# First-table blocks turned by TensorE from a ring of four whole-row tiles, and all sample tokens served by gathered rows and dots

## The reference

```python
q = (xb @ w_pq).reshape(T, PEER_HEADS, 2, D_HALF)
s = jnp.einsum('thcd,ckd->thck', q, sub_keys)
...
best, sel = lax.top_k(cand, PEER_TOPK)            # 8 heads x 16 = 128 experts of each token
eidx = jnp.take_along_axis(cidx, sel, axis=-1)
g = jax.nn.softmax(best, axis=-1)
u = jnp.take(u_tab, eidx, axis=0)                 # rows of the first table, 16384 x 2048
a = jax.nn.gelu(jnp.einsum('thkd,td->thk', u, xb))
vv = jnp.take(v_tab, eidx, axis=0)                # rows of the second table
return jnp.einsum('thk,thkd->td', g * a, vv)
```

## Time and profile before

| | |
|---|---|
| median of 3 runs | 2655.49 us (2642.95 to 2659.84) |
| the profiled execution, its own time | 2656.08 us |
| its span, first to last instruction | 2654.5 us |
| mean granted TensorE clock | 0.969 of full |
| until the first gelu of the U stage | 854.3 us |
| from the first gelu to the last (127 blocks) | 1016.5 us |
| from the last gelu of the U stage to the end | 783.7 us |

### The profile page before, as it was taken

How to read it: one execution, slowest core, us unless ns; L and a number is a source line. 1 busy time by engine, 2 the same in 40 slices (tenths; PEclk the granted TensorE clock), 3 DMA queues, 4 the chain that set the end, 5 groups by cost and what they waited for, 6 DMA issues and landing times.

```text
span 2654.5 us, 38865 instructions
## 1 busy us (share of the span) xinstructions
PE 2437.1 (92%) x13838; PEld 2178.1 (82%) x13838; DVE 1922.1 (72%) x2105; ACT 932.1 (35%) x1018; POOL 1171.8 (44%) x684
## 2 busy tenths in 40 slices
PE   5989999999799999999979898898998999999899
PEld 4878777788699999999979898898776777777777
DVE  4554654643567998989877776776588898888888
ACT  3354544522333333323322232222333333333333
POOL 1020101020000010177888888882676675767662
PEclk9999999999899999999989999998999999999999
DMA  5453544495355568689888998997899999999997
GB/s 184 132 186 112 174 129 135 150 380 190 81 119 122 163 199 224 183 230 220 212 235 231 264 245 231 237 241 202 304 390 390 399 385 411 387 391 406 394 398 301
DMA packets 280169, 661.43 MB, mean 249 GB/s; under 512 B 73145, under 2 KB 123129, under 8 KB 237912
## 3 DMA queue, kind: packets, MB, share of 16 engines
q1 hardware_dynamic: 154832, 334.57, 38.9%
q0 software_dynamic: 82064, 249.26, 27.7%
q10 hardware_dynamic: 43191, 76.58, 10.2%
HBM read 613.65 MB, written 46.02 MB: 249 GB/s over the span
## 4 chain that ended last, share of the span: by engine, by line
PE 36%; POOL 25%; DMA 15%; DVE 13%; issue 7%; DVEq 1%; ACT 1%; ACTq 1%; SPq 0%; POOLq 0%
POOL g_dense L500 16%; PE banks L1297 11%; PE banks L1298 11%; PE banks L1299 11%; POOL a_values L542 6%; DMA a_tile<-a_dense 4%; DVE h L1249 4%; DMA v_row<-in_v_tab,route_place 3%; DMA raw<-in_v_tab 3%; POOL u_row L494 2%; DMA v_raw<-in_v_tab 2%; DMA raw<-in_u_tab 2%; POOL v_row L533 1%; DVEq L847 1%; DVE u_turned L1126 1%
## 5 line engine op out<-in xcount | busy, mean ns | idle before, releaser
L1297 PE MATMUL banks<-xT_hi,ring_hi 128*128 128x320 f32 (+1 forms) x2304 | 737.2, 320 | 88.4 <-DVE ring_lo L1130 81.2
L1298 PE MATMUL banks<-xT_lo,ring_hi 128*128 128x320 f32 (+1 forms) x2304 | 731.3, 317 | 0.0
L1299 PE MATMUL banks<-xT_hi,ring_lo 128*128 128x320 f32 (+1 forms) x2304 | 730.8, 317 | 0.0
L500 POOL DMA_INDIRECT g_dense<-route,route_place x256 | 497.1, 1942 | 132.1 <-issue 76.2
L1297 PEld LDWEIGHTS banks<-xT_hi,ring_hi 128*128 128x128 f32 x2304 | 444.8, 193 | 98.6 <-issue 83.3
L1298 PEld LDWEIGHTS banks<-xT_lo,ring_hi 128*128 128x128 f32 x2304 | 444.9, 193 | 0.0
L1299 PEld LDWEIGHTS banks<-xT_hi,ring_lo 128*128 128x128 f32 x2304 | 444.1, 193 | 0.0
L533 POOL DMA_INDIRECT v_row<-in_v_tab,route_place x128 | 284.4, 2222 | 187.3 <-DVE h L1249 165.4
L868 DVE TENSOR_TENSOR ring_lo<-raw,ring_hi 128x2048 fp32r<-128x2048 f32 x72 | 164.8, 2292 | 252.7 <-ACT ring_hi L580 252.4
L1130 DVE TENSOR_TENSOR ring_lo<-u_turned,ring_hi 128x2048 fp32r<-128x2048 f32 x128 | 290.5, 2270 | 72.3 <-ACT ring_hi L785 71.8
L1126 DVE STREAM_TRANSPOSE u_turned<-raw 128x2048 f32<-128x2048 f32 x128 | 295.6, 2310 | 63.7 <-DMA raw<-in_u_tab 55.5
(11 more groups left out here) (219 smaller groups left out, 3791.6 us busy)
## 6 DMA issues: line engine op xcount, KB each, us to landing
raw<-in_u_tab SPq DMA_DIRECT2D x512, 128.0 KB
raw<-in_u_tab ACTq DMA_DIRECT2D x512, 128.0 KB
v_raw<-in_v_tab SPq DMA_DIRECT2D x64, 1024.0 KB, 10.8
raw<-in_v_tab SPq DMA_DIRECT2D x64, 1024.0 KB, 12.1
raw<-in_w_in SPq DMA_DIRECT2D x160, 256.0 KB
a_dense<-gelu_out SPq DMA_DIRECT2D x128, 160.0 KB
raw<-in_w_out SPq DMA_DIRECT2D x64, 256.0 KB
g_dense<-zeros POOLq DMA_DIRECT2D x16, 1024.0 KB, 28.9
```

What stands on the lines that cost most here:

```text
L500: pool.indirect_dma_start(out=places, out_offset=bass.IndirectOffsetOnAxis(ap=routeU[:, t, 2, j:j + 1], axis=0), in_=route[:, t, 0, j:j + ...
L1297: MM(out, h1, h2, start=first, stop=False)
L1298: MM(out, h1, l2, start=False, stop=False)
L1299: return MM(out, l1, h2, start=False, stop=last)
```

## The change

Blocks of the first table are now loaded as whole rows (8 KB a partition, one DMA a block, from SP alone) into four buffers instead of two. TensorE turns them, 16 transposes of 128x128 into four PSUM banks, in two halves of 8. They stand inside the matmuls of the block before. ACT and VectorE make the hi and lo part from PSUM, in two halves too. VectorE's `turn` and `u_turned` are gone, and with them the permuted layout of x and of `w_pq`.

The U stage's matmuls lose the 64 sample tokens: 256 columns instead of 320. All 128 sample tokens go by gathered rows: 128 gathers and 128 dots instead of 64, and no copies of x and indexes. The V stage has no `gather_gelus` left; `w_values` is made once.

GpSimd's order is new: tile 0 is routed first and its scatters begin; after 48 scatters there is one gather after every two scatters. The dots are spread over blocks 31 to 123.

```diff
-TILE_ORDER = (2, 0, 1)
-ALONE = N_SWEEPS + N_PARTS
-MIXED = ALONE + 3 * N_PARTS - 1
-GT = 64
-TU = T - GT
-DOTS = GT
+TILE_ORDER = (0, 2, 1)
+FIRST, SECOND = N_SWEEPS + N_PARTS, N_SWEEPS + 2 * N_PARTS
+TU = SEQ
+DOTS = PH * TOPK
+LAST_DOT = 124
 NUB = 3
+UR = 4
+AHEAD_ROWS = 48
...
 def dots_after(m):
-    if m < MIXED:
-        return max(m + 1 - ALONE, 0) // 3
-    done = (MIXED - ALONE) // 3
-    return min(DOTS, done + (m + 1 - MIXED) * (DOTS - done) // 66)
+    return min(DOTS, max(m + 1 - SECOND, 0) * DOTS // (LAST_DOT - SECOND))
...
-        u_v = I["u_tab"][0].rearrange("(r i q) (a d) -> a i q r d", r=4, i=32, q=P, a=4)
+        u_v = I["u_tab"][0].rearrange("(p q) d -> p q d", q=P)
...
+            def u_next(m, slot):
+                sp.wait_ge(u_turn, m * 2 + (2 - 2 * UR))
+                u_load(m, slot)
...
-            for n in range(TD // P * PH * 2):
-                t, h, half = n // (2 * PH), n // 2 % PH, n % 2
-                if n % (2 * PH) == 0:
-                    pool.wait_ge(rt_ready, t + 2)
-                if half == 0 and n:
-                    pool.wait_ge(g_scat, 16 * (n // 2 * TOPK))
-                for k in range(half * TOPK // 2, (half + 1) * TOPK // 2):
-                    scatter(t, h * TOPK + k)
-                while gathered < min(DOTS, dots_after(38 + (n + 1) * 5 // 2) + NUB):
+            for n in range(N_SCATTER // 2):
+                t, j = divmod(2 * n, SLOTS)
+                if j == 0:
+                    pool.wait_ge(rt_ready, 1 + 2 * t)
+                if j % TOPK == 0 and n:
+                    pool.wait_ge(g_scat, 16 * 2 * n)
+                scatter(t, j)
+                scatter(t, j + 1)
+                if 2 * n == AHEAD_ROWS:
+                    pool.wait_ge(rt_ready, 2)
+                if 2 * n >= AHEAD_ROWS and gathered < DOTS:
                     gather_dot(gathered)
                     gathered += 1
...
-            def gather_gelus(i):
...
             pool.wait_ge(rt_ready, NT)
+            pool.wait_ge(dot_done, DOTS)
             gather_row(0)
...
             def u_hi(m, k):
-                act.wait_ge(u_turn, m + 3)
...
+                for g in range(2):
+                    act.wait_ge(u_turn, 2 * m + g + 1)
+                    if m >= 2:
+                        act.wait_ge(u_used, m - 1)
+                    A(ringH[:, k, g * 2 * W:(g + 1) * 2 * W], psum[:, 2 + 2 * g:4 + 2 * g, :], ACT.Copy).then_inc(u_hi_done, 1)
...
-            for m in range(P - 2):
-                turn(m + 1, (m + 1) % 2)
+            for m in range(P):
                 u_lo(m, m % 2)
...
+            def u_turns(n, it, slot, g):
+                pe.wait_ge(u_in[slot], it * 16 + 16)
+                pe.wait_ge(u_lo_done, n * 2 + (g - 1))
+                for i in range(8):
+                    b = 8 * g + i
+                    last = TR(bank[2 + b // 4][:, b % 4 * P:(b % 4 + 1) * P], rawu[slot][:, b * P:(b + 1) * P], ident)
+                last.then_inc(u_turn, 1)
+
+            def u_step(m, it, q, turns=True):
                 pe.wait_ge(gelu_done, m + 1)
                 for b in range(KC):
+                    if turns and b in (2, 8):
+                        u_turns(m + 1, it + (q + 1) // UR, (q + 1) % UR, b // 8)
+                    if b % 8 == 0:
+                        pe.wait_ge(u_lo_done, m * 2 + (b // 8 + 1))
```

More of the change, by code:

```diff
@@ L278, in hybrid_layer @@
         g_zero, g_scat = sem("g_zeroed"), sem("g_scattered")
-        u_turn, gelu_done = sem("u_turn"), sem("gelu_done")
+        u_in = [sem(f"u_in{i}") for i in range(UR)]
+        u_turn, u_hi_done, u_lo_done, u_used, gelu_done = (sem(x) for x in "u_turn u_hi u_lo u_used gelu_done".split())
         a_store = [sem("a_store0"), sem("a_store1")]
@@ L338, in _, with u_load @@
                     weight_step(nb * 4 + (BASE_WOUT + i), i % 2, I["w_out"][0], kq, slice(nb * W, (nb + 1) * W))
-            pq = I["w_pq"][0].rearrange("(a b j) n -> a j b n", a=4, b=KC)
             with sp.Fori(0, 4) as nb:
                 for kq in range(4):
[L343 to L349, removed]
+                    weight_step(nb * 4 + (BASE_WPQ + kq), kq % 2, I["w_pq"][0], kq, ds(nb * W, W))
+            def u_load(m, slot):
+                sp.dma_start(rawu[slot], u_v[:, ds(m, 1), :].rearrange("p o d -> p (o d)")).then_inc(u_in[slot], 16)
+            def u_next(m, slot):
+                sp.wait_ge(u_turn, m * 2 + (2 - 2 * UR))
+                u_load(m, slot)
             def store_gelu(m, k):
@@ L354, in store_gelu @@
                 sp.dma_start(Ad[ds(m, 1), :, :].rearrange("o p x -> (o p) x"), aout[:, k, :]).then_inc(a_store[k], 16)
[L356 to L373, removed]
+            sp.wait_ge(split_used, BASE_WPQ + 2)
+            u_load(2, 2)
+            u_load(3, 3)
+            for m in range(2):
+                sp.wait_ge(lo_done, BASE_U + m + 1)
+                u_load(m, m)
+            for m in range(UR, 2 * UR):
+                u_next(m, m % UR)
+                if m >= 6:
+                    store_gelu(m - 6, m % 2)
+            with sp.Fori(2, P // UR) as it:
+                for q in range(UR):
+                    u_next(it * UR + q, q)
+                    store_gelu(it * UR + (q - 6), q % 2)
             def v_weights(m, slot):
@@ L521, in _ @@
                 gathered += 1
-            pool.wait_ge(dot_gelu, 1)
-            pool.dma_start(aval[own, 0:DOTS], adot[0:GT, :]).then_inc(aown_in, 16)
-            pool.dma_start(aval[own, DOTS:SLOTS], adot[own, :]).then_inc(aown_in, 16)
-            gelus = Ad.rearrange("m p (t o) -> (m p t) o", o=1)
             rows = I["v_tab"][0]
@@ L535, in gather_row @@
                     in_offset=bass.IndirectOffsetOnAxis(ap=routeU[:, NT - 1, 1, k:k + 1], axis=0)).then_inc(row_in[k % NVB], 16)
[L537 to L544 removed]
             pool.wait_ge(rt_ready, NT)
+            pool.wait_ge(dot_done, DOTS)
             gather_row(0)
[L548 to L553 removed]
+            pool.wait_ge(u_used, P)
             for k in range(1, SLOTS):
[L555 to L557 removed]
                 gather_row(k)
@@ L805, in _ @@
                 gelu(m, m % 2)
-                if m == P - 4:
-                    act.wait_ge(dot_done, DOTS)
-                    A(adot[:, :], adot[:, :], ACT.Gelu_apprx_tanh).then_inc(dot_gelu, 1)
-            u_hi(P - 1, 1)
-            gelu(P - 2, 0)
-            gelu(P - 1, 1)
             def v_hi(m, s, sets):
@@ L1215, in _ @@
                     dots += 1
-            turn(P - 1, 1)
-            u_lo(P - 2, 0)
-            u_lo(P - 1, 1)
             def w_product(j):
```

154 lines of the change are left out of this document (46 added, 108 removed).

## The result

The changed kernel takes 2683.73 us (median of 4 runs, 2683.65 to 2698.41), against 2654.01 for the kernel before on the same chip: the ratio is 1.0126, with a 95% interval of 1.0099 to 1.0153. It is slower by 1.3% on that ratio (the forecast was 2700, 1.7%). The profiled execution took 2683.65 us, its span is 2682.1.

What follows compares the result with a forecast made beforehand. TensorE, then VectorE's chain, bound the U stage before and transfers the V stage; GpSimd's list would bound the U stage's middle after. Span 2654.5 + 75 - 30, plus 1.6 around it, gives 2701, forecast 2700 us; 8-in-10 range 2630 to 2750.

Steps and rivals of the forecast that it cites:

- The bound: U stage, blocks 31 to 106: GpSimd's ordered list sets the pace, 9.2 us a block.
- the floor: U stage: TensorE's least time a block, 5.76 us of matmuls plus 1.76 of transposes, 7.52 us.
- Transposes cost more: Rival, U stage: transposes take 0.18 us each among fast matmuls, floor 8.7 us a block, 2757 us; chance 0.08.
- The cycle: GpSimd, middle of U stage: two scatters and a gather 4.99 us, dots 1.0, landing waits 0.5; 6.5 us a gather.
- Its place in the time: U stage timeline: first gather at 1093, 104th at 1769, end at 1946 us, 75 later than before.
- The rule on `u_lo`: U stage: `u_lo` with one input in PSUM doesn't hold GpSimd back; if wrong, up to 38 us more.
- The V stage: V stage: without small gathers in groups of eight, DMA goes at 410 GB/s instead of 393, saving 30 us.
- At nothing: The rest, costed at zero: SP's loads and four buffers, DMA demand of 275 GB/s, GpSimd's waits.
- it has 7 us to spare: SP's queue, U stage: a gelu's store stands behind a load that awaits a turning, with 7 us of slack.
- chain up: Rival, U stage: late gathers stop VectorE, TensorE idles and its clock falls; 15 to 45 us more, 2715 to 2745; chance 0.17.
- TensorE sets the pace: Rival, U stage: a GpSimd cycle under 5.46 us leaves TensorE as the limit, 2572 us; chance 0.08.

## Why the prediction was right

**The bound.** It named GpSimd's list as what sets the middle stretch, and three of the runs confirm it from three sides: another mix of the same list shortens it, wider matmuls don't lengthen it, shorter dots shorten it.

**TensorE.** 0.12 us for 256 columns and 0.11 for a transpose both hold, and so does the floor: 7.5 us a block in the first 31 blocks (7.52 said) and 7.4 in the last 21. "Transposes cost more" is out.

**The cycle.** Said: 4.99 of its own, 1.0 for the dots, 0.5 for landing, 6.5 in all. Measured: 1.2 at most for the dots, 33.3 / 103 = 0.3 for landing, 6.44 in all. A dot holds GpSimd somewhat longer than I took from the mean of all operations (a scatter begun under a dot ends 1.44 us after it in the mean, a gather 0.8 to 0.9), and the landing waits were shorter, which fits with gathers that land in 6.9 us and not in the 9.5 read before, but wasn't tried. The two errors nearly cancel, and that 6.44 lies so near 6.5 is in part luck.

**Its place in the time.** The first gather came at 1098 (1093 said), the 104th at 1761 (1769). The middle stretch had 9.1 us a block (9.2). The U stage ended 59 us later and not 75. Of these 16 us 8 are the gathers' (1769 to 1761). From the 104th gather to the 107th gelu passed 13.6 us, where 14 were said, though rows landed in 6.9 us and not in 10. The last 21 blocks took 155.4 us (1774.6 to 1930.0) where 158 and 5 for blocks with two dots were said: another 8. So the 5 us weren't needed; the terms were a little too large, and no step failed. Two readings of the rows were loose: the first 31 blocks of the kernel before took 7.5 us each by their gelus and not 7.4, and the block before block 31 ended at 1079.5 before and 1082.8 after, not at 1086 in both. The sum uses neither, as it starts from the first gather.

**The rule on `u_lo`.** The scatters beside it take 1.56 us, their own time; the 38 us kept for the rule's being wrong are not there.

**The V stage.** -31.6 us against -30, at 409 GB/s in its first 620 us for 410. (775 us by 393 / 410 are 32 us less; the forecast had rounded down to 30.) The reason given, groups of eight that hold up the large gathers, is confirmed by putting them back: 24 us for the groups, and 7 that remain when the same gathers are spread.

**"At nothing".** SP's order was rightly costed at nothing as it stands. But "it has 7 us to spare" was no full account: what it depends on is which store stands behind which load, and a ring of two without moving the stores costs 990 us.

**The clock** fell to 0.94 where I had seen 0.96 before. It didn't lengthen the stretch by anything that shows: 103 gathers of 6.44 us and the 13.6 us behind the last of them account for its end at 1774.6, so "chain up" took nothing extra. The rival "TensorE sets the pace" was sound as a condition: it wanted gathers faster than TensorE asks for them, 5.46 us with the dots in 93 blocks and 5.6 with them in 96, and the list that reaches 5.59 with 96 takes 2585.62, where I had 2572.

## What to carry to other kernels

An engine that is busy 40% of the span can set the time if its list is strictly ordered and something urgent stands in it behind things that are not: count the cycle of that list in the stretch where it is full, and try its order before its work. Count too what asks for that list's work: spreading the dots over three more blocks lowered the demand. Here the change as made costs 1.3%, the same change with another order on GpSimd and that spread is 2.5% faster than the kernel before (2585.62 and 2586.27 us), and with two loads moved on SP 2.8% (2579.6 us). When buffers in a ring are cut, follow the whole circle of load, use, result and store through each queue, since a store behind a load can close it.

## What was not expected of the hardware

An indirect DMA begun on GpSimd while VectorE runs a dot with two SBUF inputs does not only lose the rest of the dot: a scatter, which takes 1.56 us alone, ends 1.44 us after the dot's end (mean of 73), and a gather, 0.99 alone, 0.78 us after it (25), so most of either was still to be done. A subtraction with one input in PSUM and one in SBUF costs it nothing (1.56 us over 55 scatters). And the DMA engines moved 409 and 410 GB/s in the V stage when no small gathers came between, at a share of 1.02; in the best list's middle stretch they were at 0.98 too with 338 GB/s, so I would expect little more there from a still faster U stage; no run tries it.
